# Routing and gate matrix earlier, and the last 48 up-projection tiles each followed by a down-projection

## The reference, cut to what matters

```python
N_EXPERTS = 128 * 128; PEER_HEADS = 8; PEER_TOPK = 16; D_MODEL = 1024

def peer_block(xb, w_q, sub_keys, u, v):
    q = (xb @ w_q).reshape(tb, PEER_HEADS, 2, D_KEY // 2)
    s = jnp.einsum('thpc,pnc->thpn', q, sub_keys).astype(jnp.float32)
    s_top, i_top = lax.top_k(s, PEER_TOPK)
    cand_s = (s_top[:, :, 0, :, None] + s_top[:, :, 1, None, :]).reshape(tb, PEER_HEADS, PEER_TOPK * PEER_TOPK)
    cand_i = (i_top[:, :, 0, :, None] * N_KEYS + i_top[:, :, 1, None, :]).reshape(...)
    best_s, best_j = lax.top_k(cand_s, PEER_TOPK)
    expert = jnp.take_along_axis(cand_i, best_j, axis=-1)
    gate = jax.nn.softmax(best_s, axis=-1)
    pre = jnp.einsum('thkd,td->thk', u[expert], xb).astype(jnp.float32)
    act = jax.nn.gelu(pre, approximate=False) * gate
    return jnp.einsum('thk,thkd->td', act.astype(v.dtype), v[expert])
```

## Time and profile before

| | |
|---|---|
| median of 3 runs | 1876.55 us (1875.07 to 1878.01) |
| profiled execution, its own time | 1875.91 us |
| its span | 1874.1 us |
| TensorE matmuls busy | 1777.3 us, 95% |
| VectorE busy | 1434.5 us, 77% |
| ScalarE busy | 778.4 us, 42% |
| GpSimd busy | 644.6 us, 34% |
| moved by DMA | 478.22 MB |

### The profile page before, as it was taken

One profiled execution on the slowest core, in us unless ns is written; L12 is line 12 of the kernel. 1 busy time (PEld: TensorE's weight loads), 2 busy tenths in 40 slices (PEclk: granted clock), 3 DMA queues, 4 the chain that ended last, 5 costly groups with the idle time before them and its releaser, 6 DMA issues.

```text
span 1874.1 us, 26361 instructions
## 1 busy us (share of the span) xinstructions
PE 1777.3 (95%) x9675; PEld 1516.0 (81%) x9675; DVE 1434.5 (77%) x2750; ACT 778.4 (42%) x1555; POOL 644.6 (34%) x409
## 2 busy tenths in 40 slices
PE   6999999989999899999999999978999999999997
PEld 6999776559998899999899999976676666766764
DVE  4433676665678788989999999867888788888787
ACT  3112566553444333333768788522222222222222
POOL 1100000000000133434223366555557566665672
PEclk8999799789999999999999999999999999999998
DMA  6233100002222589989788899999999999999996
GB/s 217 68 131 121 45 1 1 1 1 85 68 77 95 185 305 334 316 307 327 262 276 297 279 387 387 386 400 333 386 389 382 401 387 389 401 402 384 400 379 216
DMA packets 153599, 478.22 MB, mean 255 GB/s; under 512 B 14896, under 2 KB 53808, under 8 KB 149888
## 3 DMA queue, kind: packets, MB, share of 16 engines
q1 hardware_dynamic: 96112, 264.62, 38.7%
q0 software_dynamic: 56928, 208.28, 30.4%
q10 hardware_dynamic: 432, 3.64, 0.5%
HBM read 419.47 MB, written 56.75 MB: 254 GB/s over the span
## 4 chain that ended last, share of the span: by engine, by line
PE 69%; DVE 16%; DMA 8%; ACT 3%; issue 3%; POOL 0%; SPq 0%; ACTq 0%; DVEq 0%
PE ps L1003 17%; PE ps L981 16%; PE ps L633 10%; PE ps L1012 7%; PE ps L918 5%; DMA g_in<-gates_scattered 4%; PE ps L723 3%; DVE hot L1718 3%; DVE w_lo L1339 3%; DVE ring L1737 2%; PE ps L969 2%; PE ps L714 2%; PE ps L766 2%; DMA ring<-u_rows,idx_b 1%; DMA raw<-w_tiles 1%
## 5 line engine op out<-in xcount | busy, mean ns | idle before, releaser
L981 PE MATMUL ps<-md_hi,w_hi 128*128 128x384 f32 x1024 | 358.6, 350 | 36.9 <-DVE w_lo L1339 36.7
L981 PE MATMUL ps<-md_hi,w_lo 128*128 128x384 f32 x1024 | 345.8, 338 | 0.0
L981 PE MATMUL ps<-md_lo,w_hi 128*128 128x384 f32 x1024 | 345.7, 338 | 0.0
L613 POOL DMA_INDIRECT ring<-u_rows,idx_a x128 | 197.2, 1541 | 404.2 <-DVE dots L1737 294.8
L1339 DVE TENSOR_TENSOR w_lo<-raw,w_hi 128x1024 fp32r<-128x1024 f32 x176 | 215.3, 1223 | 79.2 <-ACT w_hi L1265 59.4
L613 POOL DMA_INDIRECT ring<-v_rows,idx_a x128 | 225.1, 1759 | 136.7 <-DVE acc L1747 105.4
L1737 DVE CUSTOM_DVE_ANT_0 ring<-ring,x_n 128x1024 f32<-128x1024 f32 x192 | 230.7, 1223 | 12.7 <-DMA ring<-u_rows,idx_b 10.7
L1747 DVE SCALAR_TENSOR_TENSOR acc<-ring,actg,acc 128x1024 f32<-128x1024 f32 x188 | 234.8, 1282 | 0.0
L981 PEld LDWEIGHTS ps<-md_hi,w_hi 128*128 128x128 f32 x1024 | 194.5, 190 | 46.3 <-DVE w_lo L1339 45.3
L1003 PE MATMUL ps<-w_hi,p_hi 128*128 128x512 f32 x576 | 193.0, 416 | 9.4 <-DVE w_lo L1805 9.1
L981 PEld LDWEIGHTS ps<-md_lo,w_hi 128*128 128x128 f32 x1024 | 194.5, 190 | 0.0
(11 more groups left out here) (265 smaller groups left out, 3261.2 us busy)
## 6 DMA issues: line engine op xcount, KB each, us to landing
raw<-w_tiles SPq DMA_DIRECT2D x176, 512.0 KB, 5.2
v_buf<-v_rows SPq DMA_DIRECT2D x128, 512.0 KB, 11.4
gates_scattered<-g_st SPq DMA_DIRECT2D x24, 1024.0 KB, 6.7
g_in<-gates_scattered SPq DMA_DIRECT2D x32, 768.0 KB, 15.8
activated<-act_st SPq DMA_DIRECT2D x112, 192.0 KB, 4.2
act_in<-activated SPq DMA_DIRECT2D x28, 768.0 KB, 12.9
kv_t<-qkv ACTq DMA_DIRECT2D x3, 1184.0 KB, 4.7
xh<-x_t SPq DMA_DIRECT2D x8, 296.0 KB, 6.0
```

The source lines that it names most:

```text
L613: pool.indirect_dma_start(ring[slot][:], None, u_rows if table == "u" else v_rows, bass.IndirectOffsetOnAxis(ap=idx, axis=0)).then_inc(gat ...
L981: mm = nc.tensor.matmul(ps[:, slot, 0:ND], w[:, slot, kc, :], x[:, kc, :], start=(kc == 0 and j == 0), stop=(kc == KC - 1 and j == 2))
```

## The change

1. **Routing and gates earlier.** The 74 steps are spread over tiles 0 to 72 instead of 90 (`STEP_LINE`), the 64-token block's routing (RT_B) goes last, and the gate matrix begins at tile 28 instead of 64, so its last matmuls stand at tile 76.
2. **Fused tiles.** From up tile 81 on (`FUSED` = 80), TensorE's list holds up tile i and then down tile i - 81 (a "place"). Places 0 to 47 are tiles 80 to 127, whose activations stay on chip; places 48 to 127 are tiles 0 to 79, stored and loaded as before, and come after the last up tile. During the fused tiles the v tiles have four buffers and there is one pair of split v buffers (`vf_hi`, `vf_lo`) instead of two.
3. **Gates in groups of 8.** `GL_TILES` is 8, the quarters have 384 KB, and SyncE issues the quarters of the next group at places 0, 2, 4 and 6 of a group, again behind that place's v load.
4. **Gathered operations.** By `OP_LINE`: 55 before tile 80, 197 beside tiles 80 to 127, 132 beside the last 80 places. The ring keeps 5 slots until the up tiles are over.

```diff
-PLAN = [("top", RT_A), ("sel", RT_B), ("top", RT_B), ("top", RT_D0), ("top", RT_D1), ("sel", RT_D2), ("top", RT_D2)]
+PLAN = [("top", RT_A), ("top", RT_D0), ("top", RT_D1), ("sel", RT_D2), ("top", RT_D2), ("sel", RT_B), ("top", RT_B)]
...
-STEP_LINE = [(0, 0), (7, 13), (64, 54), (90, N_STEPS)]
-G_AT = 64
+STEP_LINE = [(0, 0), (7, 13), (24, 26), (40, 39), (56, 57), (72, N_STEPS)]
+G_AT = 28
...
-GL_TILES = 16
-DOT_LINE = [(10, 0), (64, 67), (90, 97), (112, 140), (N_EXP, 178)]
+GL_TILES = 8
+FUSED = 80
+N_FUSED = N_EXP - FUSED
+V_TILES = [*range(FUSED, N_EXP), *range(FUSED)]
+OP_LINE = [(10, 0), (28, 25), (76, 45), (FUSED, 55), (N_EXP, 252), (N_EXP + FUSED, 384)]
...
+            def beside_place(j):
+                last = min(j + 3, N_FUSED - 1) if j < N_FUSED - 1 else min(j + V_SLOTS, N_EXP - 1)
+                while len(v_asked) <= last:
+                    load_v(len(v_asked))
+                    v_asked.append(j)
...
+                if j >= N_FUSED and j % 4 == 0:
+                    sp.wait_ge(v_done, j)
+                    g = (j - N_FUSED) // 4 + 2
+                    for g in range(1 if j == N_FUSED else g, min(g + 1, FUSED // 4)):
+                        load_acts(g)
+                if j >= 0 and j % 2 == 0 and 2 <= j // GL_TILES + 1 < N_EXP // GL_TILES:
+                    sp.wait_ge(p_made, j // GL_TILES * GL_TILES)
+                    load_gates(j // GL_TILES + 1, j % GL_TILES // 2)
...
+                if i > FUSED:
+                    beside_place(i - FUSED - 1)
+            for i in range(N_FUSED - 1, N_EXP):
+                beside_place(i)
...
                 mm.then_inc(u_done, 1)
+                if i == FUSED:
+                    pe.wait_ge(g_evac, N_GRP)
+                if i > FUSED:
+                    down(i - FUSED - 1)
+            for i in range(N_FUSED - 1, N_EXP):
+                down(i)
...
             for i in range(N_EXP):
+                if i > FUSED:
+                    product(i - FUSED - 1)
                 for g in groups_of(i, 0):
                     one_hot(g)
...
+                if i > FUSED:
+                    p_low(i - FUSED - 1)
+                    v_low(i - FUSED - 1)
+                for s in ops_of(i):
                     gathered(s)
```

More of the change, by code:

```diff
@@ L1741, in gathered @@
                 if s == N_U:
-                    dve.wait_ge(v_done, KEPT // 2)
+                    for stored in g_stored:
+                        dve.wait_ge(stored, 16 * (N_GB // 2))
                 if k < 2:
@@ L1802, in v_low @@
                     dve.wait_ge(v_hi_ready, q + 1)
-                    if q >= 2:
-                        dve.wait_ge(v_done, SPLIT[q - 2] + 1)
-                    TT(v_lo[q % 2], v_buf[i % V_SLOTS][:], v_hi[q % 2].bitcast(F32), SUB).then_inc(v_ready, 1)
-            product(0)
-            product(1)
-            product(2)
-            p_low(0)
-            v_low(0)
-            p_low(1)
-            for i in range(N_EXP):
+                    before = q - (1 if i < N_FUSED else 2)
+                    if before >= 0:
+                        dve.wait_ge(v_done, SPLIT[before] + 1)
+                    hi, lo = v_parts(i)
+                    TT(lo[:], v_buf[V_SLOT[i]][:], hi[:].bitcast(F32), SUB).then_inc(v_ready, 1)
+            steps = routing()
+            for i in range(N_EXP):
+                if i > FUSED:
+                    product(i - FUSED - 1)
+                for g in groups_of(i, 0):
+                    one_hot(g)
+                if i + 1 < N_EXP:
+                    lo_part(B_U + i + 1, (i + 1) % 2, raw_u[(i + 1) % RAW_SLOTS])
+                for s in range(5):
+                    if i == GATE_TILE[s] + 1:
+                        gates_of(s)
+                if i == OP_LINE[0][0] - 2:
+                    normed_rows()
+                for _ in range(along(STEP_LINE, i), along(STEP_LINE, i + 1)):
+                    s = next(steps)
+                    if s is not None:
+                        assert GATE_TILE[s] == i, (s, i)
+                        gates_below(s)
+                if i > FUSED:
+                    p_low(i - FUSED - 1)
+                    v_low(i - FUSED - 1)
+                for s in ops_of(i):
+                    gathered(s)
+            product(N_FUSED - 1)
+            p_low(N_FUSED - 1)
+            v_low(N_FUSED - 1)
+            for j in range(3):
+                product(N_FUSED + j)
+            p_low(N_FUSED)
+            v_low(N_FUSED)
+            p_low(N_FUSED + 1)
+            for i in range(N_FUSED, N_EXP):
                 if i + 1 < N_EXP:
@@ L1819, in _ @@
                     p_low(i + 2)
[L1820 removed]
+                for s in ops_of(N_EXP + i - N_FUSED):
                     gathered(s)
[L1822 to L1828 removed]
             n_fin = 0
```

286 lines of the change are left out of this document (138 added, 148 removed).

## The result

The changed kernel takes 2010.86 us (median of 4 runs, 2007.38 to 2013.76); the kernel before took 1875.81 us beside it (1873.67 to 1878.01). The ratio is 1.072, 95% interval 1.071 to 1.074: slower by 135 us. The profiled execution took 2010.19 us with a span of 2008.4.

What follows compares the result with a forecast made beforehand. TensorE was taken to set the pace, with DMA engines full too in the down stage. Tile 80's end at 1052, plus 6, 425, 359, 7, 119 and a 13.7 us tail, gave 1983 us, range 1900 to 2070.

Steps and rivals of the forecast that it cites:

- The nine gaps: Last 80 places: TensorE idles for each late last gate quarter of groups 7 to 15, 13.3 us a group, 119 us.
- The whole stage: Last 80 places: TensorE's work 359 us, bunched first loads 7 us, late gate quarters 119 us.
- The entry: Start of the fused tiles: a burst of v tile and gate loads costs 6 us, range 0 to 13.
- Tiles 11 to 80: Up tiles before the fused ones: 380 us plus 8 lost to VectorE's coinciding routing and one-hot rows, ending at 1052.
- The fused tiles: Up tiles 81 to 127 with places 0 to 46: 425 us, range 404 to 454, at 2.2 us per operation.
- The rival that made the ring of five the bound: Fused tiles take 454 us and quarter landings stay long, L = 13: 2048 us in all, chance 0.18.
- The sentence on the Trainium skill's 358 GB/s: Fused tiles: by this HBM rate 160 MB would take 447 us instead of 425; the sum does without it.
- The tail: Work behind the last matmul: unchanged at 13.7 us.
- The first rival: Last 80 places: the late quarter is covered after all and the kernel is faster, 1823 us at best; chance 0.09.

Runs made afterwards that it cites:

- experiments 1 and 2: 1: changed kernel, gate quarters at places 0, 1, 2, 3 (1950.32 us) or 0, 2, 4, 5 (1999.55 us). 2: kernel before, last quarter at tile 14, not 9 (1947.93 us).
- experiment 3: Changed kernel, v tiles 2 and 3 and second gate group loaded later: 2004.84 us; also with no gathered operations beside tiles 76 to 81: 2013.85 us.
- experiment 5: Changed kernel with thin entry, 136 operations beside the last 80 places, quarters at places 0 to 3, groups of 16 from place 64: 1920.51 us.
- Experiment 6: Kernel before, with 6 or 12 gathered operations moved from the last 16 up tiles to the tiles before 64: 1867.41 us and 1864.54 us.

## Why the prediction was right, and where its terms were off

Slower, and the mechanism that makes it so, came out as forecast; the sum was 28 us short of the median. By its terms, in the profiled execution:

- **The nine gaps (forecast 119 us with the clock).** Measured: 103 us of gaps and some 2.3 us more for the 54 matmuls behind each, 124 us. The way was read right: the cover is the 5.15 us of one place, the landing 7.3 to 10.5 us in eight of nine gaps (9 was taken), the 6.4 us on VectorE exact. The reason given for the short landing, that TensorE's idle time drains the queues, is only half of it: TensorE still works for 4.7 us of the landing, and it is VectorE and GpSimd that stand throughout (experiments 1 and 2). The last gap, 18.71 us, has a landing of 13.63 us: five loads of `h_fin` for the tail, 8.25 us of issuing, stand ahead of it in SyncE's list. The whole stage took 486.5 us (485 forecast): its bare work was 5 us shorter, since split tiles ran at 4.10 instead of 4.18 us.
- **The entry (forecast 6 us, range 0 to 13).** Measured: 19.8 us of idle time before place 0 and 2.6 us more for place 0, which took 6.79 us at a granted clock of 0.62 (1092.8 to 1099.6). This is one mis-sized term. I priced the bytes by the former burst, and left out that SyncE itself stands while it issues a burst. By experiment 3 the fetches beside these tiles make most of it.
- **Tiles 11 to 80 (forecast 8 us lost, at most 17).** Measured: tile 80's Gelu at 1067.33 instead of 1052, 23 us lost. This is the other mis-sized term. From 664 to 1067 TensorE waits 13.6 us for `w_lo` (13 times, the longest 2.2), mostly behind VectorE's routing and one-hot rows, and once 2.8 us for ScalarE's one-hot rows. By the Gelus, the tiles from 28 to 76 lost 17.9 us, the top of the forecast's range. I had scaled VectorE's load per tile and not the order in its list, in which one long step delays a split. Tiles 12 to 27 took 71.3 us (66.7 before), some 5 lost that the prediction put at nothing: a routing block now ends there, and `w_lo` waits behind ScalarE's part of it. This I read from the trace alone; no run tried it.
- **The fused tiles (forecast 425 us).** Measured: 418 us, up tile 81 included, with TensorE busy for 405.56 of 415 us and the queues at 373 GB/s. The rival that made the ring of five the bound, at 454 us, is out; but 415.3 us are 2.15 for each of the 193 operations, close to the 2.2 that were taken, and experiment 5 shows the stage growing with them. The sentence on the Trainium skill's 358 GB/s for a core ("DMA: Bandwidth & Descriptors", Specifications, as half of a stack's 716) fares as the prediction had it: the trace shows 373 GB/s over 415 us here, and 395 before.
- **The tail** took 13.8 us (13.7 forecast).

The late place of the last quarters explains about half of the 135 us: 60.5 us by the medians, and 71 of the stage in the profiled executions, went when the quarters moved (415 against 486.5 us). The rest is deeper than the prediction put it. The first rival, that with the quarter covered the kernel would be faster, finds no support: even with five sixths of the last gates not loaded the kernel stays at 1.011. As I read the windows, the change takes bytes out of the one stage with room (664 to 1067 ran at 254 GB/s, a share of 0.74, where the kernel before has 302 and 0.88) and adds them to stages whose queues are full. An overlap that would free TensorE is then paid in landings. Experiment 6 is the same account from the other side.

## What to carry to other kernels

For every load that a whole group waits for, add up issue, landing and the consumer's list, and compare it with the work that lies between the issue and the first use; a smaller buffer can leave much less of it (27 us became 5 here). Where the DMA engines are full, take the landing from the state that the edit will make, not from the state it is read in: here it was shorter while the engines that ask for rows stood, and longer once the gaps closed. Before two stages are laid over one another, look at the bytes of each per window, and move bytes into the window that has room; a few gathered operations there were worth more than the whole overlap.

## What the runs showed of the hardware

- Issuing costs the issuing queue's time when transfers pile up: four 384 KB quarters took 22.28 us to issue behind four v tiles and gathered fetches, 15.27 with two v tiles fewer, 4.22 with the fetches gone too.
- The landing went by what else was under way more than by size: 64, 192 and 384 KB needed a median of 10.4, 11.4 and 13.8 us in the same places, while 768 KB needed 5.6 to 9.0 us with VectorE and GpSimd standing and 24.7 us in a full stage.
